# Eight experts in the body of the expert loop instead of two

## The reference

```python
def moe_ffn(h, router_w, router_b, w_gate_up, b_gate_up, w_down, b_down):
    logits = (h @ router_w).astype(jnp.float32) + router_b.astype(jnp.float32)
    top_logit, top_idx = lax.top_k(logits, TOP_K)          # 4 of 32 experts for each token
    gate = jax.nn.softmax(top_logit, axis=-1)
...
    def expert_block(args):
        xe, e = args
        gu = xe @ w_gate_up[e] + b_gate_up[e]              # 1024 -> 2048
        gt, up = jnp.split(gu, 2, axis=-1)
        gt = jnp.minimum(gt, SWIGLU_LIMIT)
        up = jnp.clip(up, -SWIGLU_LIMIT, SWIGLU_LIMIT)
        act = (up + 1.0) * (gt * jax.nn.sigmoid(SWIGLU_ALPHA * gt))
        return act @ w_down[e] + b_down[e]                 # 1024 -> 1024
...
    return jnp.einsum('nk,nkd->nd', gate.astype(y.dtype), y)
```

## Time and profile before

| what | value |
|---|---|
| runs of the kernel | 1682.2, 1682.44 and 1687.22 us; median 1682.44 us |
| profiled execution, first to last instruction | 1684.8 us |
| TensorE busy | 1441.6 us (86%), 6338 matmuls |
| VectorE busy | 489.9 us (29%) |
| ScalarE busy | 216.7 us (13%) |
| HBM, read and written | 264 GB/s over the span |
| the expert loop on TensorE | from 460 to about 1667 us of the span |

### The profile page before, as it was taken

The page is one execution under the profiler, slowest core; times in us unless marked ns, Lnnn a source line. Parts: engine busy times, 40 slices in busy tenths (PEclk is TensorE's granted clock), DMA queues, the critical chain, the costliest instruction groups (busy, mean ns, idle before and its releaser), DMA issues.

```text
span 1684.8 us, 17303 instructions
## 1 busy us (share of the span) xinstructions
PE 1441.6 (86%) x6338; PEld 670.7 (40%) x6339; DVE 489.9 (29%) x1237; ACT 216.7 (13%) x364; POOL 36.5 (2%) x44
## 2 busy tenths in 40 slices
PE   6997999989797977979788979779797887979786
PEld 4674677964332322323222323223232332323222
DVE  1694644335521311212131213212121221213123
ACT  2111432101101111011111011110111101011102
POOL 3120010000000000000000000000000000000000
PEclk9998998879698989989898989999898988989899
DMA  9657210133849798797918897987979779797921
GB/s 248 136 94 98 100 50 1 51 115 151 319 164 417 316 392 331 306 416 310 406 54 362 329 416 305 372 346 314 414 290 416 305 321 400 307 417 311 366 93 53
DMA packets 83060, 446.92 MB, mean 265 GB/s; under 512 B 6225, under 2 KB 7137, under 8 KB 50001
## 3 DMA queue, kind: packets, MB, share of 16 engines
q1 hardware_dynamic: 79600, 435.88, 67.0%
q0 software_dynamic: 2720, 7.13, 1.8%
q10 hardware_dynamic: 576, 1.31, 0.3%
HBM read 439.92 MB, written 4.39 MB: 264 GB/s over the span
## 4 chain that ended last, share of the span: by engine, by line
PE 83%; issue 9%; DMA 4%; DVE 2%; ACT 2%; ACTq 0%; DVEq 0%; SPq 0%
PE ps L1008 27%; PE ps L1019 15%; PE ps L665 8%; PE ps L982 6%; PE ps L1026 6%; PE ps L1003 5%; DMA arena<-in_w_main 2%; PE ps L883 2%; DMA arena<-in_b_gate_up 1%; PE ps L876 1%; PE ps L770 1%; PE ps L704 1%; PE ps L990 1%; PE ps L649 1%; PE ps L1084 1%
## 5 line engine op out<-in xcount | busy, mean ns | idle before, releaser
L1008 PE MATMUL ps<-arena 128*64 128x512 f32 (+1 forms) x2176 | 480.0, 602 | 0.0
L1008 PEld LDWEIGHTS ps<-arena 128*64 128x64 f32 (+1 forms) x2176 | 174.4, 139 | 303.2 <-issue 303.2
L1019 PE MATMUL ps<-arena 128*64 128x512 f32 (+1 forms) x1088 | 258.7, 608 | 19.1 <-ACT arena L605 17.5
L1491 DVE TENSOR_SCALAR arena<-ps 128x512 f32<-128x512 f32 (+1 forms) x34 | 23.5, 693 | 849.4 <-PE ps L1008 849.4
L1003 PE MATMUL ps<-arena 128*64 128x512 f32 (+1 forms) x272 | 105.3, 842 | 139.3 <-issue 138.2
L665 PE MATMUL ps<-arena 128*128 128x320 f32 x576 | 160.9, 442 | 18.9 <-DMA arena<-in_w_main 13.3
L1019 PEld LDWEIGHTS ps<-arena 128*64 128x64 f32 (+1 forms) x1088 | 85.1, 138 | 166.9 <-issue 165.1
L665 PEld LDWEIGHTS ps<-arena 128*128 128x128 f32 x576 | 111.7, 195 | 67.7 <-issue 23.6
L982 PE MATMUL ps<-arena 128*64 128x512 f32 (+3 forms) x420 | 114.3, 609 | 8.7 <-DMA arena<-in_b_gate_up 4.8
L1026 PE MATMUL ps<-arena 128*128 128x512 f32 (+3 forms) x228 | 101.9, 605 | 3.8 <-ACT arena L588 1.4
L598 ACT ACTIVATE arena<-arena 128x512 f32<-128x512 f32 x32 | 20.2, 632 | 658.3 <-DVE arena L1491 658.3
(11 more groups left out here) (280 smaller groups left out, 1008.0 us busy)
## 6 DMA issues: line engine op xcount, KB each, us to landing
arena<-in_w_gate_up SPq DMA_DIRECT2D x128, 2048.0 KB, 24.7
arena<-in_w_down SPq DMA_DIRECT2D x64, 2048.0 KB, 12.5
arena<-in_w_main SPq DMA_DIRECT2D x40, 512.0 KB, 3.6
arena<-in_w_merge_out SPq DMA_DIRECT2D x1, 3072.0 KB, 10.1
arena<-in_w_conv_out POOLq DMA_DIRECT2D x1, 2048.0 KB, 13.2
arena<-in_w_delta_out SPq DMA_DIRECT2D x1, 2048.0 KB, 8.4
out_delta_s<-arena POOLq DMA_DIRECT2D x1, 2048.0 KB, 18.8
arena<-in_xT SPq DMA_DIRECT2D x1, 1280.0 KB, 7.1
```

Of the source, the lines that this page charges most:

```text
L1008: m = pe.matmul(outs[q], tokens[:, k % 4, k // 4], w[:, k, q * 512:(q + 1) * 512], start=False, stop=(k == KD - 1))
L1019: m = pe.matmul(ps[slots * c:slots * (c + 1), 2, :], actT[:, k % 4, a:a + slots], dn[:, k, c * 512:(c + 1) * 512], start=(k == 0), stop=(k ...
```

## The change

The loop on TensorE, ScalarE and VectorE gets eight experts in its body and four passes in place of two experts and sixteen passes. `p` is still the expert's parity (which of two buffers it uses), `e` its number, and `two` the number of its pair, which was the loop's counter before. SyncE's loop is unchanged. The same work is done for each expert, in the same order, with the same semaphores and counts.

```diff
+BODY = 8
...
-            with act.Fori(0, E // 2) as i:
-                for p in range(2):
-                    e = 2 * i + p
+            with act.Fori(0, E // BODY) as i:
+                for w in range(BODY):
+                    p, e, two = w % 2, BODY * i + w, BODY // 2 * i + w // 2
...
-            with pe.Fori(0, E // 2) as i:
-                for p in range(2):
-                    e = 2 * i + p
+            with pe.Fori(0, E // BODY) as i:
+                for w in range(BODY):
+                    p, e, two = w % 2, BODY * i + w, BODY // 2 * i + w // 2
...
-                       gu[p], [(sem(f"ld_gu{p}_{r}"), 16 * i + 16) for r in range(4)], sem("h_mm"))
+                       gu[p], [(sem(f"ld_gu{p}_{r}"), 16 * two + 16) for r in range(4)], sem("h_mm"))
...
-                        pe.wait_ge(sem("added"), 6 * i + 2)
+                        pe.wait_ge(sem("added"), 6 * two + 2)
...
-                    down_ready = 3 * i + (3 if p else 1)
+                    down_ready = 3 * two + (3 if p else 1)
...
-            with dve.Fori(0, E // 2) as i:
-                for p in range(2):
-                    e = 2 * i + p
+            with dve.Fori(0, E // BODY) as i:
+                for w in range(BODY):
+                    p, e, two = w % 2, BODY * i + w, BODY // 2 * i + w // 2
...
-                        add(0, sem("c_mm"), sem("added"), i)
+                        add(0, sem("c_mm"), sem("added"), two)
```

More of the change, by code:

```diff
@@ L1554, in _ @@
                     if p == 0:
-                        add(0, sem("c_mm"), sem("added"), i)
+                        add(0, sem("c_mm"), sem("added"), two)
                     move_x(xg[1 - p], SLOTS, sem("xg_mm"), sem("xg_ready"), e + 2)
                     if p == 0:
-                        add(1, sem("c_mm"), sem("added"), i)
-                        add(2, sem("c_mm"), sem("added"), i)
+                        add(1, sem("c_mm"), sem("added"), two)
+                        add(2, sem("c_mm"), sem("added"), two)
                     later = dve.value_load(flags[0:1, bass.ds(e * LATER, 1)], min_val=0, max_val=1)
```

## The result

The median went from 1682.3 to 1581.5 us; the ratio is 0.940, 95% interval 0.937 to 0.943. That lies in the forecast range and 8 us under the forecast of 1589. The profiled executions have spans of 1684.8 and 1575.8 us, 109.0 us apart, which is more than the 100.8 us between the medians: the one before is the slowest of its four runs (1687.22 us), the one now the fastest of its four (1578.03 us, some 2.2 us over its span).

A forecast was written before the change was run, and what follows sets the result against it. TensorE was taken to bound the kernel, with code-fetch stalls at the ends of passes. Terms of -134.7 + 21.3 + 23 + 10 - 12.6 = -93.0 us took 1682.4 to 1589 us; 8-in-10 range 1550 to 1632.

The forecast's parts named there:

- Step 1: Ends of passes on TensorE: twelve of fifteen branches back go, with their holes and cold restarts; 134.7 us off.
- Step 2: Long forward jump alone behind TensorE's experts: stalls partly uncovered, adding 21.3 us at odd experts and 23 at even ones.
- Step 3: TensorE's clock falling in new holes of 2 us: 10 us added for 22 holes, bounds 0 and 46.
- the rival of cooled holes: Each new TensorE hole cools the clock: 36 us more than Step 3, about 1625 us; chance 0.17, with longer stalls.
- Step 4: Three remaining branches back on TensorE: the jump before them stalls some 2 us, not 6; 12.6 us off, bounds 0 and 18.
- Step 5: VectorE's branch back stalls some 7 us, three times, hidden by slack: no cost; 21 us without that cover.
- Step 6: Weight stream in the loop: needs 60.8 us of a pair's 65, so 94% full; no term.
- The rival in which the weight stream becomes the bound: Forward jumps are covered, so the stream's 60.8 us limits each pair of experts: about 1545 us; chance 0.15.

The follow-up runs named there:

- The two runs that differ by 13 instructions: Kernel before, with 205 or 192 fulfilled waits put ahead of TensorE's loop to move its body: 1531.0 us with 205, 1738.8 us with 192.
- the two fillers: Kernel before, with 51 or 25 never-run matmuls jumped over ahead of TensorE's loop: 1509.9 us with 51, 1695.5 us with 25.
- the short jump: Kernel before, bodies of two, without TensorE's code for the loop over blocks beyond the first late one: 1513.7 us (same cut in the changed kernel: 1529.1 us).
- the run with 205 waits: Kernel before, whole, with 205 long-fulfilled waits ahead of TensorE's loop so that its body lies in 7 pieces: 1531.0 us.
- the short filler: Kernel before, whole, with 25 never-run matmuls jumped over ahead of TensorE's loop, so that its body lies in 8 pieces: 1695.5 us.

## Why the prediction was right, and what in it was not

The mechanism of the sum held, term by term, and the sizes were near:

- Step 1, twelve holes with cold restarts gone: shown by the chain and by the body of eight on TensorE alone.
- Step 2, new holes at the long jump. At w1 to w4 and w6 as counted, 1.6 to 2.0 us each. Two sizes were off. At w5 the jump was taken to stall and was covered (1.88 us), four times 1.9 us too much; by the count its target lies within a few instructions of a border. At even experts I had 2.3 us, since I read the array's cover as 4.0 us; it is 4.4 there too (I had taken the end of `down` from a row of the chain at which the next matmuls already overlap), and the holes are 1.8.
- Step 3, the clock: 10 us were put in for it. Behind 16 of the 17 holes of about 2 us the restart took 15.67 us, as at w2 above. Behind one the clock fell, to 0.90 over the restart, and it took 2.72 + 14.64 = 17.36 us. So 1.7 us were lost, and the rival of cooled holes is out. That one hole, in the chain and in the columns of the earlier trace rows:

```profile
682.85 1.96 issue
684.81 2.72 PE ps L1004 x8
687.53 14.64 PE ps L1009 x64
...
684.80:702.20 17.40, 17.39 (x74) 6.95 (x76) 0.00 (x0) 0.00 (x0) 0.00 (x0) 0.90 1.00 392
```

- Step 4: the three holes that stay were taken as 5.2 us; they are 5.18, 6.76 and 6.69.
- Step 5, VectorE's stall at its branch back, hidden: right, but it is not where I looked. The branch itself takes 0.056 us as before; the stall, as I read it, stands behind it, as 6.14 us of idle time:

```profile
706.29 0.76 DVE L1487 TENSOR_TENSOR arena<-ps,arena 128x256 f32<-128x256 f32 x2 [0.41 <-PE ps L991]
713.20 0.70 DVE L1468 TENSOR_SCALAR arena<-arena 128x64 f32<-128x64 f32 x3 [6.14 <-issue]
```

  The second queue of instruction packets, q14, has 55 in place of 10, and 56 with bodies of eight on VectorE and ScalarE alone, which fits a fetch. No wait of TensorE for VectorE came of it, and that run's time was the same as before.
- Step 6, the stream at 94%: the DMA engines are at 0.98 to 1.01, nearer to the bound than I had it, and no wait for weights came of it.

Together: 22 holes of 2.0 and three of 5.2 us, 60 us, were forecast; 50.1 in 23 waits came, 17 of them holes of 1.6 to 2.0 us. That is 10 us less. TensorE's busy time was to fall by 15 us (25 for the restarts less 10 for the clock) and fell by 20.8, another 6. These 16 us are what lies between the 93.0 us forecast and the 109.0 between the two spans. That the medians show a miss of 8 us only is luck: I worked from the rows of the slowest of four runs and took the difference off their median, and the profiled execution of now is the fastest of four.

What failed is a step beside the sum. I set the Trainium skill's room of 2,048 instructions for TensorE (Runtime: NRT & Kernel Launch, Instruction fetch mechanics) against the 7.3 us of line 1068 and said that the rows disagree. They don't have to: 2,048 are eight blocks of 256. The body of 1,775 touched eight by the count, and the packets say that a ninth came with each pass. The two runs that differ by 13 instructions, the two fillers and the short jump agree with the rule. I had laid the pieces over the code for the jumps and never asked how many of them the memory keeps. The sum did not suffer, since it took the stall of the old body from its rows, whatever the reason for it. The consequence is larger than the prediction's error: read rightly, it points to a change worth 172 us, and the one made here is worth 101.

The Trainium skill says in the same section that a taken branch to a target outside the present two pages stalls for a fetch. That agrees with the jumps of line 1102, 5.9 us at the median, in a body that is fetched anyway. In a body that stays inside, jumps of 426 instructions and the branch back over all 1,775 take 0.21 us (the run with 205 waits), so on TensorE it is not two pages that are kept.

The rival in which the weight stream becomes the bound was put at 1545 us, with three ends of passes still in it. The kernels without any fetch get to 1510 with the stream full, but TensorE has no wait for weights in them and is nearly full itself; which of the two is the bound there is not shown.

## What to carry to other kernels

When a loop's branch back takes microseconds, count the instructions of its body as the chip runs them (a float32 matmul is four), add the code that is only jumped over, and see how many pieces of 256 it touches where it lies: shorten or move the body until it stays (here, on TensorE, seven pieces did and eight did not), before making it longer. Where it can't fit, few passes and short forward jumps are the next best. And before a small change to a kernel with such a loop is judged by its time, look at the number of code packets: code ahead of the loop that never runs moved this kernel between 1510 and 1696 us, and waits that do nothing between 1531 and 1739.

## What was not expected of the hardware

- A loop of 1,775 instructions ran with 19 packets of code in the whole kernel or with 154, by where it begins; the times were 1509.9 us (with 51 matmuls of filler) and 1682.3 us.
- A branch record on VectorE does not show what looks like its fetch stall (0.056 us, with 6.14 us of idle time behind), while one on TensorE does (7.1 us).
- A fetch behind a jump took about 6 us on TensorE while weights streamed, and about 3.5 us where transfers rested (the jump behind the first expert with the short filler). These are different jumps; no run changed the traffic alone.
- 205 fulfilled waits in a row took TensorE's sequencer some 22 us, about 0.11 us each, though a record of one says 0.051:

```profile
L1057 PEldq EVENT_SEMAPHORE  x204: 51/51/51, 440.2 to 462.2; - x102
```
